# Wider matmul records for 36 more weight tiles, a smaller second top-16 search, and gelu one tile later

## The reference

```python
for l in range(DEPTH):                                  # 2 layers
    h = rmsnorm(x, attn_norm_gain[l]); proj = h @ w_in[l]
    q, k, v, pz, gu, gv, g = split(proj)
    gates = sigmoid(g + b_gate[l])                      # 3 branches x 1024
    ya, yb, yc = attention(q, k, v) @ wa, pool(pz) @ wb, gmlp(gu, gv) @ wc
    x = x + (gates[0] * ya + gates[1] * yb + gates[2] * yc) @ w_out[l]
    h2 = rmsnorm(x, ffn_norm_gain[l])
    # PEER: 8 heads, 128 x 128 experts
    q = h2 @ w_query                                    # 2048 columns
    s1, s2 = q[..., 0] @ keys1.T, q[..., 1] @ keys2.T   # 128 scores each
    v1, i1 = top_k(s1, 16); v2, i2 = top_k(s2, 16)
    top, ci = top_k(v1[:, None] + v2[None, :], 16)      # of 256 sums
    idx = i1[ci // 16] * 128 + i2[ci % 16]; gate = softmax(top)
    x = x + sum(gate * gelu(h2 . expert_u[idx]) * expert_v[idx])
return rmsnorm(x, final_gain)
```

## Time and profile before

| | |
|---|---|
| median of 3 runs | 2029.18 us (2028.71 to 2030.1) |
| the profiled execution | 2028.88 us, of which the span in the trace is 2027.0 us |
| PE busy | 2004.3 us of the span |
| DVE busy | 1488.2 us |
| ACT busy | 1061.8 us |
| POOL busy | 1029.8 us |
| granted TensorE clock | 0.996 of full speed |

### The profile page before, as it was taken

One profiled execution on the slowest core, in us unless ns is written; L12 is line 12 of the kernel. 1 busy time (PEld: TensorE's weight loads), 2 busy tenths in 40 slices (PEclk: granted clock), 3 DMA queues, 4 the chain that ended last, 5 costly groups with the idle time before them and its releaser, 6 DMA issues.

```text
span 2027.0 us, 39960 instructions
## 1 busy us (share of the span) xinstructions
PE 2004.3 (99%) x12788; PEld 1819.2 (90%) x12788; DVE 1488.2 (73%) x3096; ACT 1061.8 (52%) x1746; POOL 1029.8 (51%) x425
## 2 busy tenths in 40 slices
PE   9999999999999999999999999999999999999998
PEld 7999998899999888888889999888999998888887
DVE  2855169988887888888639450799888878888886
ACT  5644555567776333333466444555677753333333
POOL 6898779787775000000278988798777740000001
PEclk8999999999999999999999999999999999999999
DMA  8355557675666787878774556676666567787775
GB/s 256 129 194 188 183 186 235 212 226 198 197 195 195 244 239 242 242 240 242 240 208 143 192 174 199 194 235 215 213 197 199 197 203 243 240 241 241 241 242 175
DMA packets 172128, 429.62 MB, mean 212 GB/s; under 512 B 19156, under 2 KB 83957, under 8 KB 171510
## 3 DMA queue, kind: packets, MB, share of 16 engines
q1 hardware_dynamic: 171588, 425.56, 66.5%
q10 hardware_dynamic: 434, 2.63, 0.3%
HBM read 392.79 MB, written 35.32 MB: 211 GB/s over the span
## 4 chain that ended last, share of the span: by engine, by line
PE 93%; DVE 3%; issue 1%; POOL 1%; ACT 1%; DMA 1%; DVEq 0%; POOLq 0%; ACTq 0%; SPq 0%
PE bank L1300 40%; PE bank L1563 33%; PE bank L1549 9%; PE bank L1551 5%; PE bank L1614 3%; POOL halves L545 1%; PE bank L1529 1%; DVE area L1155 0%; DVE area L1159 0%; DVE area L1162 0%; PE bank L1439 0%; DMA ring<-in_stream 0%; PE bank L1395 0%; DVE act L1235 0%; DMA x<-in_x 0%
## 5 line engine op out<-in xcount | busy, mean ns | idle before, releaser
L545 POOL TENSOR_TENSOR halves<-ring,halves 128x1024 fp32r<-128x1024 f32 x412 | 1024.2, 2498 | 975.7 <-DVE coef L1243 683.0
L626 ACT ACTIVATE halves<-ring 128x1024 fp32r<-128x1024 f32 x668 | 705.2, 1057 | 684.7 <-PE bank L1563 414.1
L1300 PE MATMUL bank<-hT,halves 128*128 128x256 f32 x6048 | 751.8, 283 | 1.9 <-DVE hT L921 1.7
L1300 PEld LDWEIGHTS bank<-hT,halves 128*128 128x128 f32 x6048 | 737.2, 192 | 4.4 <-DVE hT L921 2.1
L1563 PE MATMUL bank<-halves,coef 128*128 128x512 f32 x3000 | 681.5, 389 | 0.0
L1563 PEld LDWEIGHTS bank<-halves,coef 128*128 128x128 f32 x3000 | 562.7, 188 | 117.4 <-issue 0.5
L1223 DVE TENSOR_TENSOR halves<-ring,halves 128x1024 fp32r<-128x1024 f32 x256 | 315.5, 1233 | 12.7 <-ACT halves L626 10.2
L1549 PE MATMUL bank<-hT,halves 128*128 128x512 f32 x896 | 312.2, 395 | 3.0 <-POOL halves L545 3.0
L1551 PE MATMUL bank<-hT,halves 128*128 128x256 f32 x896 | 248.6, 277 | 0.0
L1549 PEld LDWEIGHTS bank<-hT,halves 128*128 128x128 f32 x896 | 168.1, 188 | 42.7 <-issue 3.6
L1551 PEld LDWEIGHTS bank<-hT,halves 128*128 128x128 f32 x896 | 168.3, 188 | 0.0
(11 more groups left out here) (168 smaller groups left out, 1375.0 us busy)
## 6 DMA issues: line engine op xcount, KB each, us to landing
ring<-in_stream SPq DMA_DIRECT2D x668, 512.0 KB, 4.0
held_blocks<-act SPq DMA_DIRECT2D x244, 128.0 KB, 1.8
act<-held_blocks SPq DMA_DIRECT2D x244, 128.0 KB, 3.0
area<-rel_scratch SPq DMA_DIRECT2D x16, 128.0 KB, 5.4
area<-in_gains SPq DMA_DIRECT2D x4, 512.0 KB, 4.1
x_home<-x ACTq DMA_DIRECT2D x2, 1024.0 KB, 4.2
x<-x_home SPq DMA_DIRECT2D x2, 1024.0 KB, 8.0
area<-in_params SPq DMA_DIRECT2D x2, 640.0 KB, 7.6
```

The source lines that it names most:

```text
L545: pool.tensor_tensor(halves[:, s, 1, :], ring[:, s, :], halves[:, s, 0, :].bitcast(F32), ALU.subtract)\
L626: a.activation(halves[:, s, 0, :], ring[:, s, :], ACT.Copy).then_inc(hi_done, 1)
L1300: i = pe.matmul(o, stationary[a], moving[b], start=begin and n == 0, stop=end and n == len(TERMS) - 1)
```

## The change

Three things:

- The 20 gate tiles of sets 1 to 5 and the 16 query tiles of each layer use the form of `sided` (a new helper, `sided_columns`). Each takes a whole bank; DVE adds the sides (a tensor_reduce per tile). For the gates DVE writes the sum to `sig`, and ACT's sigmoid then works in place on SBUF. Gate set 0 stays as it was. ACT no longer takes the query results.
- The second search looks at 112 of the 256 sums (4 rows of 16 and 12 rows of 4, which is enough for the 16 largest). Ranks are found with four scalar_tensor_tensor instructions, and turned into expert numbers by 16 masks per side, each of 256 elements (comparison and multiplication in one), and two reductions of 2048 elements. Between the folds there are 7 folds here instead of 12, and the rest of the folds come in a row after it.
- In the parked stage ACT rounds tile b+4 and then does the gelu of tile b-1, not b. The exp comes at turn 10, not 11, one place later within the turn.

```diff
-EXP_AT = 11
+EXP_AT = 10
+WIDE = 4
+NARROW = 4
+CAND = WIDE * TOPK + (TOPK - WIDE) * NARROW
@@ ACT, gates(n)
                     for k in range(2):
                         high_up_to(T_GATE[n] + 2 * k + 1 + 3)
...
+                        if n == 0:
+                            b = group("gate")
                         for c in range(2):
...
+                            into = sig_of(n)[:, 2 * k + c, :]
+                            if n > 0:
+                                a.wait_ge(taken_v, l * NGV + taken_before(place("sum", 4 * (n - 1) + 2 * k + c) + 1)[0])
+                            i = a.activation(into, b[:, c * S:(c + 1) * S] if n == 0 else into, ACT.Sigmoid, bias=par[:, col:col + 1])
@@ ACT, parked stage
+                def next_high(r, s):
                     a.wait_ge(tiles_used, l * NT + r * RING + (T_PU + s + 1))
                     high(r * RING + (T_PU + RING + s), s)
-                    park(r, s)
+                def turn(r, s):
+                    next_high(r, s)
+                    if s > 0:
+                        park(r, s - 1)
+                    else:
+                        park_last(r)
@@ DVE, mix
+                def add_gates(n):
...
+                    for k in range(4):
+                        b = group("sum")
+                        v.tensor_reduce(sig_of(n)[:, k, :], b[:, :].rearrange("p (e t) -> p t e", e=2), AX.X, ALU.add)\
+                            .then_inc(taken_v, 1)
                 for hf in range(2):
                     for br in range(BR):
+                        if 3 * hf + br < 2 * BR - 1:
+                            add_gates(3 * hf + br + 1)
                         for n in range(2):
                             b = group("branch")
@@ DVE, query
+                g[0] = first("qq")
+                for n in range(2 * PH):
+                    b = group("qq")
+                    v.tensor_reduce(qqT[:, n // 2, n % 2, :], b[:, :].rearrange("p (e t) -> p t e", e=2), AX.X, ALU.add)\
+                        .then_inc(taken_v, 1)
@@ DVE, ranks to numbers
-                for c, rank in ((0, caf), (1, cbf)):
-                    for t in range(TT):
-                        link(v.tensor_tensor(eq, rank[:, t].unsqueeze(3).to_broadcast([P, PH, TOPK, TOPK]),
-                                             iota[:, 0:TOPK].unsqueeze(1).unsqueeze(1).to_broadcast([P, PH, TOPK, TOPK]),
-                                             ALU.is_equal))
-                        fold()
-                        link(v.tensor_tensor(eq, eq, idf[:, t, :, c, :].unsqueeze(2).to_broadcast([P, PH, TOPK, TOPK]),
-                                             ALU.mult))
-                        fold()
-                        link(v.tensor_reduce(sel[:, c, t].rearrange("p (h j) -> p h j", h=PH), eq, AX.X, ALU.add))
-                        fold()
+                for o, z in zip((c0, c4, c2), flat):
+                    i = v.tensor_copy(o, z)
+                link(i)
+                fold()
+                link(v.scalar_tensor_tensor(caf, c2, float(WIDE - WIDE * TOPK // NARROW), c4, ALU.add, ALU.max))
+                v.scalar_tensor_tensor(c4, caf, -float(TOPK), c0, ALU.mult, ALU.add)
+                link(v.scalar_tensor_tensor(c2, caf, -float(NARROW), c0, ALU.mult, ALU.add))
+                link(v.scalar_tensor_tensor(cbf, c2, float(WIDE * NARROW - WIDE * TOPK), c4, ALU.add, ALU.max))
+                for c, rank in ((0, caf), (1, cbf)):
+                    for r in range(TOPK):
+                        numbers = idf[:, :, :, c, r].rearrange("p t h -> p (t h)").unsqueeze(2).to_broadcast([P, TT * PH, TOPK])
+                        i = v.scalar_tensor_tensor(eq[:, r, :].rearrange("p (h j) -> p h j", j=TOPK), rank.rearrange("p (h j) -> p h j", j=TOPK),
+                                                   float(r), numbers, ALU.is_equal, ALU.mult)
+                        if r % 6 == 5:
+                            fold()
+                    link(i)
+                    for t in range(TT):
+                        i = v.tensor_reduce(sel[:, c, t], eq[:, :, t * P:(t + 1) * P].rearrange("p r j -> p j r"), AX.X, ALU.add)
+                        if t == 0:
+                            fold()
+                    link(i)
@@ PE
+                def sided_columns(n, o, second=None):
+                    w = tile(n, KD)
+                    for k in range(KD):
...
+                        one = pe.matmul(o[:, :].rearrange("p (e t) -> p e t", e=2), w[:, 0, k], hT[:, :, k], start=k == 0, stop=False,
+                                        skip_group_check=True)
+                        i = pe.matmul(o[:, 0:S], w[:, 1, k], hT[:, 0, k], start=False, stop=True, skip_group_check=True)
```

97 lines of the change are left out of this document (58 added, 39 removed).

## The result

The changed kernel took 2069.36 us (median of 4 runs, 2062.93 to 2071.31), the kernel before 2029.64 us (median of 4, 2028.71 to 2030.52): a ratio of 1.019, 95% interval 1.0167 to 1.0213. Slower is right; the size lies outside the range of 2026 to 2055. The profiled execution took 2071.31 us, its span is 2069.5 us, 42.5 us more than before.

The account below looks back on a forecast made before the run. PE, busy for 99% of the span, was taken as the bound. 2028.88 - 7.7 (tiles) - 3.7 (pauses) + 7.0 (mix) + 16.0 (DVE's stretch) = 2040.5, with 0.3 against the median about 2041 us; range 2026 to 2055.

Parts of the forecast that it names:

- The loop of store and load: Parked stage: the later gelu delays store, load and rounding; 5.6 us estimated per pass, counted 0, at most 2 us a layer.
- The work between fold 40 and fold 47: Parked stage, DVE: folds, SBUF instructions, 32 masks, four reductions x 2.3 and closing; together 29.4 us for seven tiles.
- fold 40: Parked stage: first fold behind the casts that wait for POOL, forecast 8.2 us after the start of fold 39.
- The wait at the mix: Second branch tile of set 0: sigmoids wait for DVE's additions, so PE stands 3.5 us, twice: +7.0 us.
- a rival with a chance of 0.15: PE's long waits make the clock fall; four waits at half of 4.7 us each give 2050, up to 2060; chance 0.15.
- the forecast case: PE waits both at the second branch tile and in the parked stage: 2031 to 2050 us, chance 0.56.
- The shorter tiles: Gate and query tiles: 72 tiles at 2.773 instead of 2.88 us, 7.7 us less if PE stays fed.
- The sign that was named for it: PE waits in the first 40 parked tiles would mean the store and load order costs more than counted.
- DVE's stretch: Parked stage, tiles 44 to 51: PE waits for DVE's late folds, 8.0 us a layer, +16.0 us in two.
- Z: Parked stage: the start of fold 39, taken as 379.77 us, from which later folds were forecast.
- The pauses: Parked stage: 1.5 us for POOL and 0.34 us before the 55th tile leave, twice: 3.7 us less.
- Worth nothing: Smaller second search: it saves DVE time before fold 39, where DVE already waited 1.55 us for PE; no gain.

Follow-up runs that it names:

- E3: The changed kernel with the gelu order of the kernel before; 1.0142 of the kernel before, +28.8 us.
- E9: The kernel before with the gelu one tile behind and the store one tile behind as well; 1.0011 of the kernel before, +2.2 us.
- E8: E2 with five folds a side instead of three among the masks and reductions; 1.0047 of the kernel before, +9.5 us.
- E4: The changed kernel with the 16 masked values of a result side by side in memory; 1.0169 of the kernel before.
- E7: E1 with 28 extra matmuls keeping PE busy ahead of the wait at B1, the second branch tile; 1.0018 of the kernel before, +3.7 us.
- E6: E1 with DVE's additions of gate set 1 moved between the mixer halves; 0.9989 of the kernel before, -2.2 us.
- E5: The kernel before with the gelu one tile behind and nothing else; 1.0043 of the kernel before, +8.7 us.
- E2: The kernel before with the smaller second search and its masks alone; 1.0119 of the kernel before, +24.2 us.
- E12: The changed kernel with the edits of E6, E8, E4 and E9 together; 1.0011 of the kernel before, +2.2 us.
- E13: E12 with eight folds fewer in the second search, seven a side behind it, exp at turn 8; 0.9963 of the kernel before, -7.5 us.
- E1: The kernel before with the wider gate and query tiles alone; 1.0034 of the kernel before, +6.9 us.
- E14: E13's fold and exp edits on the kernel with the smaller search alone, old tiles and gelu order; 1.001 of the kernel before, +2.0 us.
- E10: E8 with the values of a result side by side in memory as in E4; 1.0047 of the kernel before.

## Why the prediction was wrong in size, step by step

The profiled execution took 2071.3 us where the sum said 2040.5. Two steps failed above all. The loop of store and load, counted at 0, took 10.6 us by the trace and 9.7 by E3. The work between fold 40 and fold 47, taken as 29.4 us with "four reductions x 2.3", took 35.4 and 34.4: 11.0 us more in the two layers, 8.3 with the 0.2 and 2.5 us by which fold 40 came earlier than forecast. The clock behind the waits at B1 (3.7 us), the slower pace of the wide and parked tiles (2.6 and 2.3) and one query tile at half clock (1.5) stood in no term. That is 29 of the 30.8 us; the splitting is by the profile. What runs tested are the loop (E3, E9), the spread of the folds (E8), the length of a reduction (E4) and the clock (E7); that the slower pace costs what is put down here is reckoned, not tested.

**The wait at the mix** (+3.5 a layer): right in chain, place and size (3.3 us in both layers; DVE free at 106.85 against 107.2, B1 at 112.2 against 112.5). E6 shows the cause. Not in the sum: the clock behind it, 2.4 and 1.3 us. It stood as a rival with a chance of 0.15 and half of 4.7 us for each wait, which came out as the size of a whole fall, by luck: nothing in the prediction says why half. The mistake was to set it beside the forecast case as another outcome, when it is a consequence of the waits that the forecast itself contained. That the clock "stays at full speed" after the many short pauses was no evidence on a wait of twice their length.

**The shorter tiles** (-7.7): mis-sized. 2.773 us was read in one stretch of eight tiles and taken for all. After a wait the same tile often runs at 2.826 us until the next disturbance; in the profile of after 23 of the 72 tiles ran at 2.773, so the term was 23 x 0.107 + 49 x 0.054 = 5.1 us, and layer 2's parked tiles lost 44 x 0.053 = 2.3 us of it again. In layer 1 the first query tile also took 4.42 us instead of 2.91, at a granted clock of 0.57 from 220 to 224 us. The additions of the query tiles were free, as counted.

**"I count 0" for the store and load loop** (upper end 2 us a layer): the step that failed in kind, a wait put at nothing. The loop was written down correctly, and with the estimate of 5.6 us against 5.546 for two tiles it came out even on paper. In the trace the pairs of folds are 5.7 us apart (376.48 and 382.22), and fold 39 comes 2.8 and 2.0 us later behind its tile than in before. Alone the new order costs 8.7 us (E5), of which the store one tile behind gives back 6.5 (E9). In the changed kernel it put the 2.8 and 2.0 us in front of DVE's stretch, and 1.5 and 4.3 us behind it; giving the order up takes 9.7 us out (E3). The sign that was named for it, waits of PE in the first 40 parked tiles, would hardly have told: PE loses 0.6 us there in layer 1 (tiles 36 to 39) and nothing in layer 2, since the loop first eats the lead.

**DVE's stretch** (+8.0 a layer): right that the first fold behind the ranks and the thin spread of folds decide (E8). Fold 40 was right to 0.2 us in layer 1 by luck: the shift did not wait (0.28 us), the differences did (1.82 us instead of 0.59), and two casts did; in layer 2 it came at Z + 5.7, 2.5 us early, and in E2 and E3 at Z + 4.6. Mis-sized was "four reductions x 2.3": 3.83 us each, +6.2 us, since the new view reads with a step that L1162 did not have. The SBUF instructions took 3.9 us instead of 1.7, because one met POOL (2.65 us against 0.42). Masks at 0.33 instead of 0.40 us gave 2.1 back. Together 35.4 instead of 29.4 us. With fold 39's lag that makes 8.0 - 0.2 + 6.0 + 2.8 = 16.6 of the 17.4 us of layer 1, and in layer 2, where the parked tiles ran at the slower pace, 8.0 - 2.5 + 5.0 + 2.0 + 2.3 = 14.8. The rule on GpSimd and VectorE that the prediction cited from the Trainium skill ("SBUF — State Buffer", section "SBUF: two separate sides") held: the three casts took 5.11 us here and 0.70 us in E3, where POOL stood idle from 386.8 to 388.8.

**The pauses** (-3.7): the 1.5 us for POOL went, but where it went alone (E9) it was no gain, because DVE holds PE before tile 54 instead, for 2.3 us.

**"Worth nothing" for the smaller search**: right for the kernel as changed, and the wrong question. Time was there, in DVE's waits for PE before the folds of the search (13.5 us in 60 in E12), and E13 turns it into 9.7 us against E12, by three edits that were not separated.

Left open: what decides between 2.773 and 2.826 us a tile, and when a wait of 3.5 us makes the clock fall and when not; and how much of E9's 2.2 us is such chance.

## What to carry to other kernels

Work that is moved from one place to another in an engine's written order must be followed through every queue that runs in step with it: here the gelu was moved and its store was not, and the load behind the store stopped ACT. Folding a second engine's duty into long work needs the longest piece between two duties to stay under the lead of the engine that waits, and a reserve earned earlier only helps if the order lets the engine run ahead. Before a duration is carried over from a similar row, compare how the operands step through memory, and if the forecast contains a wait on PE as long as the 3.5 us here, put the clock behind it into the same sum.

## What the hardware did that was not expected

- One wait, at one place, 3.45 to 3.47 us in E1, E3, E4 and the changed kernel (two layers each): once the matmuls behind it started 0.12 us apart, three times 0.18 on average over the tile, four times 0.213 to its end. In layer 2 of E3 nine matmuls behind the wait ran at full speed before the slow ones began, so the fall can come a microsecond after PE has started again.
- A tile of `sided` has two stable paces, 2.773 and 2.826 us, with the same instructions. In the slow one the narrow matmul starts 0.233, 0.241 and 0.236 us behind the wide one before it, in turn, in the fast one 0.230 to 0.233. In these traces the pace changes only after a pause. In E1 layer 1's parked stage ran in the one and layer 2's in the other.
- From gate set 1 to the first score matmul kernels with before's code take 166.6 us, 168.1 (layer 2 of E5, layer 1 of E14) or 169.6 (layer 1 of E5, E8, E9 and E10). Where it is longer, PE stands 1.3 us more at the transposes of the second norm; in the longest the first query tile behind takes 4.43 us instead of 2.95, at half clock for most of it. Stretches of E8, before and behind the start of that tile (216.29):

```profile
206.00:216.00 10.00, 7.30 (x38) 5.44 (x37) 7.61 (x10) 5.35 (x13) 5.18 (x2) 1.00 0.33 105
216.00:220.00 4.00, 3.71 (x18) 3.74 (x19) 0.85 (x2) 1.95 (x3) 2.92 (x2) 0.57 0.64 262
```

So the clock can also fall after several short waits of PE close together (1.3 us and less each). This and the paces may well be the spread of before from 2027.6 to 2035.9 us.
- A DVE reduction of 2048 elements takes 2.27 to 2.29 us read side by side and 3.76 to 3.93 us with a step of 1 KB; masks of 256 elements start 0.33 us apart, and 0.45 to 0.47 us when they write with a step of 64 bytes.
